# A two-layer mixer kernel: rotated scan states summed on GpSimd before the read, compression with its positions stationary, and four heads' weights per transpose

## What is computed

```python
z = rmsnorm(h, norm_mix) @ w_in              # q, six key/value parts, gates, u
kc, vc = compress(k_cmp, ...), compress(v_cmp, ...)
p_cmp = masked_softmax(q @ kc * scale)       # 31 compressed positions
o = g0 * (p_cmp @ vc) + g1 * o_slc + g2 * o_win

def compress(kv, pe, w1, w2):                # 31 windows of 32 tokens, 2 groups
    return gelu((windows(kv) + pe) @ w1) @ w2   # 2048 -> 256 -> 64

# S5 branch: 32 groups of 16 channels, 64 complex states each
state = scan(a_bar, b_coef * (b @ u))
y = real(state) @ c_re - imag(state) @ c_im + d_skip * u
h = h + concat(o, y_gated) @ w_out
```

## Time and profile before

| | |
|---|---|
| median of 3 runs | 2008.1 us (2006.92 to 2008.7) |
| profiled execution | 2005.77 us, span 2004.0 us |
| granted clock, mean | 0.985 |
| PE, PEld busy | 1936.8 us (97%), 1509.8 us (75%) |
| DVE, ACT, POOL busy | 1185.7 us (59%), 820.9 us (41%), 336.2 us (17%) |
| HBM read | 192.67 MB, 97 GB/s over the span |

### The profile page before, as it was taken

How to read it: one execution, slowest core, us unless ns; L and a number is a source line. 1 busy time by engine, 2 the same in 40 slices (tenths; PEclk the granted TensorE clock), 3 DMA queues, 4 the chain that set the end, 5 groups by cost and what they waited for, 6 DMA issues and landing times.

```text
span 2004.0 us, 22537 instructions
## 1 busy us (share of the span) xinstructions
PE 1936.8 (97%) x9022; PEld 1509.8 (75%) x9022; DVE 1185.7 (59%) x1519; ACT 820.9 (41%) x1210; POOL 336.2 (17%) x329
## 2 busy tenths in 40 slices
PE   7999999999998999999999899999999899999997
PEld 5788888777644788888888778776788778776786
DVE  5748344576764556656655787826753659446732
ACT  5332233311555343213333448545542466445531
POOL 2000000135320110101011212504201024115002
PEclk9999999999998999999999899999999899999998
DMA  5232223222002145645632222221223222221331
GB/s 196 93 106 94 93 96 116 78 74 97 27 1 69 55 151 195 221 141 185 215 111 80 77 93 85 87 95 40 74 95 95 85 82 84 89 80 32 95 98 60
DMA packets 53464, 197.27 MB, mean 98 GB/s; under 512 B 6000, under 2 KB 6512, under 8 KB 52848
## 3 DMA queue, kind: packets, MB, share of 16 engines
q1 hardware_dynamic: 43200, 160.55, 24.4%
q0 software_dynamic: 7648, 29.10, 4.6%
q10 hardware_dynamic: 2512, 6.18, 0.9%
HBM read 192.67 MB, written 2.10 MB: 97 GB/s over the span
## 4 chain that ended last, share of the span: by engine, by line
PE 78%; DVE 13%; ACT 4%; issue 2%; POOL 2%; DMA 1%; ACTq 0%; POOLq 0%; DVEq 0%
PE PS L593 77%; DVE AR L1644 3%; DVE WLO L1641 2%; DVE AR L2170 1%; ACT WHI L1179 1%; DVE AR L1674 1%; DVE TMP L2244 1%; DVE AR L1995 1%; PE PS L843 1%; DVE AR L2137 0%; DMA H<-in_xT 0%; POOL ACC L2302 0%; DVE H L2073 0%; POOL AR L2339 0%; ACT SQ L1194 0%
## 5 line engine op out<-in xcount | busy, mean ns | idle before, releaser
L593 PE MATMUL PS<-HNH,WHI 128*128 128x512 f32 x1632 | 659.3, 404 | 16.4 <-ACT HNH L1210 14.6
L1641 DVE TENSOR_TENSOR WLO<-RAW,WHI 128x1024 fp32r<-128x1024 f32 (+1 forms) x272 | 374.9, 1381 | 506.7 <-ACT WHI L1179 506.6
L593 PE MATMUL PS<-HNH,WLO 128*128 128x512 f32 x1632 | 641.8, 393 | 5.9 <-DVE WLO L1641 5.9
L1179 ACT ACTIVATE WHI<-RAW 128x1024 fp32r<-128x1024 f32 (+1 forms) x272 | 297.7, 1095 | 642.2 <-PE PS L593 583.1
L593 PE MATMUL PS<-HNL,WHI 128*128 128x512 f32 x1632 | 436.3, 391 | 0.1
L593 PEld LDWEIGHTS PS<-HNH,WHI 128*128 128x128 f32 x1632 | 309.1, 189 | 96.3 <-issue 22.1
L593 PEld LDWEIGHTS PS<-HNH,WLO 128*128 128x128 f32 x1632 | 309.5, 190 | 80.4 <-issue 9.1
L593 PEld LDWEIGHTS PS<-HNL,WHI 128*128 128x128 f32 x1632 | 307.6, 188 | 64.8 <-DVE HNL L1644 1.0
L2302 POOL TENSOR_TENSOR ACC<-ACC,SQ 128x512 f32<-128x512 f32 x46 | 62.4, 1356 | 809.8 <-ACT SQ L1194 808.8
L593 PE MATMUL PS<-AR 32*128 32x256 f32 (+14 forms) x844 | 162.3, 414 | 4.4 <-POOL AR L2339 1.7
L593 PE MATMUL PS<-HIDH,WLO 128*128 128x512 f32 x352 | 137.1, 390 | 0.0
(11 more groups left out here) (314 smaller groups left out, 2295.4 us busy)
## 6 DMA issues: line engine op xcount, KB each, us to landing
RAW<-in_w_in SPq DMA_DIRECT2D x80, 512.0 KB, 3.5
AR<-in_w_ada POOLq DMA_DIRECT2D x48, 512.0 KB, 4.1
RAW<-in_w13a SPq DMA_DIRECT2D x44, 512.0 KB, 3.4
RAW<-in_w13b SPq DMA_DIRECT2D x44, 512.0 KB, 3.6
RAW<-in_w_out SPq DMA_DIRECT2D x40, 512.0 KB, 3.5
RAW<-in_w2a SPq DMA_DIRECT2D x16, 704.0 KB, 4.0
RAW<-in_w2b SPq DMA_DIRECT2D x16, 704.0 KB, 5.1
RAW<-in_w_inA SPq DMA_DIRECT2D x12, 512.0 KB, 3.4
```

What stands on the lines that cost most here:

```text
L593: return pe.matmul(o, l, r, start=start, stop=stop, skip_group_check=True)
L1179: act.activation(hi_of(name, i), raw_of(name, i), ACT.Copy).then_inc(*HI.up(name, i))
L1641: dve.tensor_tensor(lo_of(name, i), raw_of(name, i), f32(hi_of(name, i)), S_).then_inc(*LO.up(name, i))
```

## The change

The scan: behind the second `back_v` of each b, POOL adds SQ onto V_, real halves first (`state_re`), imaginary halves second (`state_im`), each over both state tiles (128x2x256). PE's `read` then has two rounds of four matmuls, the first behind `state_re` and the second behind `state_im`. `back` of DVE and POOL no longer waits for PE's read of the b before.

The compression: the 62 positions are the stationary operand, in two column groups (PSUM partitions 0 to 61 and 64 to 125) for the two halves of the weight, which is the moving operand with 128 columns; one bank instead of two. ACT's GELU writes `HIDt`, a new step `hidden` transposes it by two PE matmuls and ACT copies it to `HIDc`. `compressed` for the values comes one n later and writes VC four times, at partitions 0, 32, 64 and 96, with four ACT copies.

The transposes: `ptc` is done for two pairs of heads at once (i = 0 and 2), four transposes of 128 columns into one bank and one ACT copy; `cmp` takes its rows from the partitions 32 x (2 (i % 2) + hf).

The ring of banks turns otherwise from the first `squeeze` on; `out_s5` passes over bank 7.

```diff
     yield "v", z, tt
     if z == 0 and tt < 2:
         yield "turn", 6 + tt
+    if (z, tt) == (0, 1):
+        yield "hidden", 0
     yield from some(1)
 if z == 0:
     yield "compressed", 0
...
 if n < 4:
     yield "squeeze", 1, n
 if n == 4:
+    yield "hidden", 1
+if n == 5:
     yield "compressed", 1
 if 1 < n < 9:
     yield "weigh", n - 2
...
+CET = [CEf.rearrange("p (q a c) -> p q a c", q=4, a=2)[:, :, a, :] for a in range(2)]
...
+HIDt = ar(20800, P)
...
 ps, bY = take(pe, "read", b)
 pe.wait_ge(*V.at("s5_thru", 3))
 mm(ps[slice(64 - r.start, 128 - r.start), 0:HT], THRU[r, y4, r], U[r, y4, 0:HT], True, False)
-for z in range(4):
+for z, (name, wr, wl) in enumerate((("state_re", CpR, CaR), ("state_im", CpI, CaI))):
+    pe.wait_ge(*G.at(name, b))
     for now in (True, False):
         for j in range(2):
             t16 = 2 * b + j
             g = t16 % 4 if now else (t16 + 2) % 4
             o = ps[32 * g:32 * g + 32, 0:HT]
-            wr, wi = (CpR, CpI) if now else (CaR, CaI)
-            if z == 0:
-                pe.wait_ge(*V.at("back_im", t16))
-                w, x = wr, S5T[j][:, HT:T]
-            elif z == 1:
-                pe.wait_ge(*G.at("back_re", t16))
-                w, x = wi, S5T[j][:, 0:HT]
-            elif z == 2:
-                pe.wait_ge(*G.at("back_v", t16))
-                w, x = wr, V_[b % 2][:, j, 0:HT]
+            x = V_[b % 2][:, j, HT * z:HT * z + HT]
+            if now:
+                t = mm(o, wr[:, t16, :], x, z == 0, z == 1)
             else:
-                w, x = wi, V_[b % 2][:, j, HT:T]
-            if now:
-                t = mm(o, w[:, t16, :], x, z == 0, z == 3)
-            else:
-                t = mm(o[:, 1:HT], w[:, t16, :], x[:, 0:HT - 1], False, z == 3)
+                t = mm(o[:, 1:HT], wl[:, t16, :], x[:, 0:HT - 1], False, z == 1)
 t.then_inc(*P_.up("read", b))
 give(bY, V, "read", b)
...
 elif step == "squeeze":
     z, c = at_
     if c == 0:
-        hc_banks[z] = [take(pe, "squeeze", z, mt) for mt in range(2)]
+        hc_banks[z] = take(pe, "squeeze", z)
     name = ("wk1", "wv1")[z]
     w = rows(raw_of(name, c), 256)
     pe.wait_ge(*raw_in(name, c))
     pe.wait_ge(*V.at("positions", z))
-    for mt in range(2):
-        for i in range(4):
-            ii = 4 * c + i
-            t = mm(hc_banks[z][mt][0][:, 0:62], w[:, i, P * mt:P * mt + P],
-                   XBp[:, ii, :, :].rearrange("p g c -> p (g c)"), ii == 0, ii == 15)
+    for i in range(4):
+        ii = 4 * c + i
+        for mt in range(2):
+            t = mm(hc_banks[z][0][64 * mt:64 * mt + 62, 0:P], XBp[:, ii, :, :].rearrange("p g c -> p (g c)"),
+                   w[:, i, P * mt:P * mt + P], ii == 0, ii == 15)
     t.then_inc(*P_.up(name, c))
     if c == 3:
-        for mt in range(2):
-            give(hc_banks[z][mt][1], A, "hidc", z, mt)
+        give(hc_banks[z][1], A, "hidt", z, 1)
+elif step == "hidden":
+    z, = at_
+    for mt in range(2):
+        ps, b = take(pe, "hidden", z, mt)
+        r = slice(64 * mt, 64 * mt + 62)
+        pe.wait_ge(*A.at("hidt", z, mt))
+        pe.transpose(ps[:, 0:62], HIDt[r, :], IDENT[r, r]).then_inc(*P_.up("hidden", z, mt))
+        give(b, A, "hidc", z, mt)
...
 for g in range(2):
     for mt in range(2):
-        t = mm(ps[0:31, 64 * g:64 * g + 64], HIDc[:, mt, 31 * g:31 * g + 31], WV2[:, mt, :], mt == 0, mt == 1)
+        for a in range(2):
+            r = 32 * g + 64 * a
+            t = mm(ps[r:r + 31, 64 * g:64 * g + 64], HIDc[:, mt, 31 * g:31 * g + 31], WV2[:, mt, :], mt == 0, mt == 1)
...
     t.then_inc(*P_.up("shares", i, kind))
     give(b, A, "shares", i, kind)
     out_bank[i, kind] = take(pe, "values", i, kind)
-if part == 0 and kind == 2:
-    for hf in range(2):
-        ps, b = take(pe, "ptc", i, hf)
-        pe.wait_ge(*V.at("weigh", 6))
-        for qt in range(4):
-            t = pe.transpose(ps[0:31, P * qt:P * qt + P], CE[:, qt, 2 * i + hf, 0:31], IDENT)
-        t.then_inc(*P_.up("ptc", i, hf))
-        give(b, A, "ptc", i, hf)
+if part == 0 and kind == 2 and i % 2 == 0:
+    ps, b = take(pe, "ptc", i // 2)
+    pe.wait_ge(*V.at("weigh", 6))
+    for qt in range(4):
+        t = pe.transpose(ps[:, P * qt:P * qt + P], CET[i // 2][:, qt, :], IDENT)
+    t.then_inc(*P_.up("ptc", i // 2))
+    give(b, A, "ptc", i // 2)
 if part == 1 and kind == 2:
     ps, b = take(pe, "cmp", i)
     pe.wait_ge(*A.at("compressed", 1))
     for hf in range(2):
-        pe.wait_ge(*A.at("ptc", i, hf))
-        t = mm(ps[64 * hf:64 * hf + 64, :], VC[0:31, 64 * hf:64 * hf + 64], PTC[hf][0:31, :], True, True)
+        pe.wait_ge(*A.at("ptc", i // 2))
+        r = slice(32 * (2 * (i % 2) + hf), 32 * (2 * (i % 2) + hf) + 31)
+        t = mm(ps[64 * hf:64 * hf + 64, :], VC[r, 64 * hf:64 * hf + 64], PTC[i // 2][r, :], True, True)
     t.then_inc(*P_.up("cmp", i))
     give(b, V, "with_cmp", i)
...
 elif step == "out_s5":
     for m in range(3):
+        if ring[0][0] == 7:
+            ring.append(ring.pop(0))
         w_out_banks[m] = take(pe, "w_out", m)
         w_out(m, (4, 5, 6, 7), True, False)
...
     for mt in range(2 if c == 3 else 0):
         act.wait_ge(*P_.at(("wk1", "wv1")[z], 3))
-        if z:
-            act.wait_ge(*P_.at("compressed", 0))
-        act.activation(HIDc[:, mt, 0:62], bank("squeeze", z, mt)[:, 0:62], ACT.Gelu_apprx_tanh).then_inc(*A.up("hidc", z, mt))
+        r = slice(64 * mt, 64 * mt + 62)
+        act.activation(HIDt[r, :], bank("squeeze", z)[r, 0:P], ACT.Gelu_apprx_tanh).then_inc(*A.up("hidt", z, mt))
+elif step == "hidden":
+    z, = at_
+    for mt in range(2):
+        act.wait_ge(*P_.at("hidden", z, mt))
+        act.activation(HIDc[:, mt, 0:62], bank("hidden", z, mt)[:, 0:62], ACT.Copy).then_inc(*A.up("hidc", z, mt))
 elif step == "compressed":
     z, = at_
     act.wait_ge(*P_.at("compressed", z))
     if z == 0:
         act.activation(KCC[:, 0:62], bank("compressed", 0)[:, 0:62], ACT.Copy).then_inc(*A.up("compressed", 0))
     else:
-        act.activation(VC[0:31, :], bank("compressed", 1)[0:31, 0:128], ACT.Copy).then_inc(*A.up("compressed", 1))
+        for g in range(2):
+            for a in range(2):
+                r = slice(32 * g + 64 * a, 32 * g + 64 * a + 31)
+                act.activation(VC[r, 64 * g:64 * g + 64], bank("compressed", 1)[r, 64 * g:64 * g + 64], ACT.Copy).then_inc(*A.up("compressed", 1))
...
-for hf in range(2 if kind == 2 else 0):
-    act.wait_ge(*P_.at("ptc", i, hf))
-    if i:
-        act.wait_ge(*P_.at("cmp", i - 1))
-    act.activation(PTC[hf][0:31, :], bank("ptc", i, hf)[0:31, :], ACT.Copy).then_inc(*A.up("ptc", i, hf))
+if kind == 2 and i % 2 == 0:
+    act.wait_ge(*P_.at("ptc", i // 2))
+    act.activation(PTC[i // 2], bank("ptc", i // 2)[:, :], ACT.Copy).then_inc(*A.up("ptc", i // 2))
...
 dve.wait_ge(*V.at("scan", b, 1))
 if b < 7:
     dve.wait_ge(*G.at("drive_im", t16 + 2))
-if b:
-    dve.wait_ge(*P_.at("read", b - 1))
 stt(f2(S5T[j][:, HT:T]), f2(V_[b % 2][:, j, HT:T]), -1.0, tables(t16, 2)[1], M_, M_).then_inc(*V.up("back_im", t16))
...
 pool.wait_ge(*V.at("scan", b, 1))
 if b < 7:
     pool.wait_ge(*G.at("drive_im", t16 + 2))
-if b:
-    pool.wait_ge(*P_.at("read", b - 1))
+else:
+    pool.wait_ge(*G.at("state_im", b - 1))
 pool.tensor_tensor(f2(S5T[j][:, 0:HT]), f2(v[:, 0:HT]), s2, M_).then_inc(*G.up("back_re", t16))
 mine()
 pool.wait_ge(*V.at("back_im", t16))
 pool.tensor_tensor(f4(v), f4(v), c4, M_).then_inc(*G.up("back_v", t16))
+if j:
+    v, turned = V_[b % 2], SQ[:, :, :]
+    mine()
+    for z, name in enumerate(("state_re", "state_im")):
+        x = v[:, :, HT * z:HT * z + HT]
+        pool.tensor_tensor(x, x, turned[:, :, HT - HT * z:T - HT * z], A_).then_inc(*G.up(name, b))
```

More of the change, by code:

```diff
@@ L330, in program @@
         RAW = sb("RAW", NSLOT * SLOT)
-        NAR = 20800
+        NAR = 20928
         at_ar = at[0]
```

## The result

| | before | after |
|---|---|---|
| median of the runs, us | 2007.5 | 2027.9 (4 runs, 2024.1 to 2030.0) |
| ratio, 95% interval | 1 | 1.0101 [1.0085, 1.0116] |
| span of the profiled execution, us | 2004.0 | 2025.5 |
| granted clock, mean over the span | 0.985 | 0.975 |
| PE busy, us | 1936.8 (97%) | 1933.9 (95%) |

The change makes the kernel 20 us slower. Slower was forecast, but 2027.9 lies above the range's 2024. PE did not gain its "some 10 us" of busy time: 140 matmuls fewer took 2.9 us less.

A forecast was written before the change was run, and what follows sets the result against it. PE, busy 97% of the span, was taken as the bound, but POOL's products set the end at five of eight reads. Terms gave +5.4 us, plus 3.5 for the clock: +8.9 on the median 2008.1, so 2017.0, range 1998 to 2024.

The forecast's parts named there:

- bank of read 2: Read 2 waits for the bank DVE frees with turn 6 and ends at 496.7 instead of 493.8: +2.9 us.
- lower clock behind the waits: PE's waits at reads 1, 2, 6, 7 could lower the clock, 1.75 us each; two of four counted: +3.5.
- the sums' own time in PE's path, read halved: PE waits for two POOL adds per read: +0.9 at read 0, +9.8 for five reads, -0.5 at reads 3, 4.
- POOL's additions slow DVE, and the clock with it: Sixteen adds could slow DVE by up to 12.8 us; only two beside positions counted, 1.6 within read 2's bank.
- the array's part, its saving: Six shorter squeezes -4.8 us, fewer transposes -3.1, added work +0.6, drive 7's short bank wait swallowed -0.4.
- The term for read 0: With the sums read 0 ends at 442.4 against 441.6 now, stated as +0.9 us.
- all four waits: By the skill's text the clock falls at reads 1, 2, 6 and 7 alike: +7.0 us instead of +3.5.
- the adds are hidden: Rival, faster: the DVE and POOL chain moves forward with PE, which finds the sums ready; 1995 to 1998 us; chance 0.20.
- bank and clock don't bite: Rival, same: turn 6's bank in time, DVE not slowed, clock unaffected by 3 us waits; +2.5, 2010.6 us; chance 0.20.
- the clock falls each time: Rival, slower: the clock falls after all four waits, reads 1, 2, 6, 7; +12.4, 2020.5 us; chance 0.15.
- the column groups of squeeze run one after the other: Rival, slower: squeeze's two column groups don't overlap, so its saving is 0; 2022 us; chance 0.05.
- what would show it: Profile signs: PE waits 12 to 18 us for adds, squeezes 1.1 us, PE busy some 10 us less, clock below 1.

The follow-up runs named there:

- experiment 9: Changed kernel with the bank ring turned two places before read 2 and accumulating matmuls in all PE waits for the sums: 2015.9 us, 1.0053.
- experiment 10: Changed kernel without the sums, ring turned before read 2, plus two unread POOL additions behind each b from 0 to 6: 2007.6 us, 1.0005.
- 5: Changed kernel with only the ring of PSUM banks turned by two places before read 2: 2024.8 us, 1.0084.
- 7: Changed kernel without the sums (read of before) and with the bank ring turned two places before read 2: 1999.2 us, 0.9962.
- Experiment 8: Kernel before with the read's matmuls halved, no sums added, part of the state left out of y: 2007.2 us, 1.0007.
- 3: Kernel before plus two POOL additions of 128x512 that nobody reads, behind the last product of each b from 0 to 6: 2014.3 us, 1.0041.
- experiment 6: Changed kernel with matmuls with a start flag in PE's waits for the sums, read 2's bank wait left: 2020.9 us, 1.0068.
- Experiment 2: Kernel before with only the sums on POOL and the halved read: 2026.3 us, 1.0098.
- experiment 1: Changed kernel without the sums, read of before; the new squeeze and four heads per transpose stay: 2006.2 us, 0.9998.

## Why the prediction was too low

The runs make a ladder from the changed kernel to the best one, each step the difference of two ratios, beside the terms of the sum. The step from 9 to 10 takes the sums out of the read, with PE's waits and the matmuls in them, and leaves as many additions on POOL (fourteen for sixteen) that nobody reads. Each step is uncertain by 4 to 5 us (the last by 2.5), so the first isn't clear of noise:

| step | runs | measured, us | forecast, us |
|---|---|---|---|
| bank of read 2 | after to 5 | 3.4 | 2.9 |
| lower clock behind the waits | 5 to 9 | 6.2 | 3.5 |
| the sums' own time in PE's path, read halved | 9 to 10 | 9.6 | 0.9 + 9.8 - 0.5 = 10.2 |
| POOL's additions slow DVE, and the clock with it | 10 to 7 | 8.6 | 0, but for 1.6 inside the bank's term |
| the array's part, its saving | 7 to before | -7.6 | -4.8 - 3.1 + 0.6 - 0.4 = -7.7 |
| together | | 20.2 | 8.9 |

**What held.** That PE doesn't find the sums done, and roughly the size of it: the third step is within its error of what was forecast. It is a mixed step, though. The matmuls in the waits keep the mean clock at 0.985 in experiment 9, and without them experiment 10 has 0.982. What is clean is the step from 9 to 7, both at 0.985 and without the late bank: 18.3 us for the sums, own time and contention together, where the forecast has 10.2 and 1.6. The split of it into 9.6 and 8.6 is not. At most reads an addition takes 1.25 to 1.36 us, against 1.27 in the sum. At read 1 the two took 3.46, since WLO and the scans run beside them (0.9 us that the sum didn't have). Squeeze took 1.09, as forecast, four heads' weights 0.66 where half of 1.06 was taken, and two small transposes 0.27; the worth of it all, 7.6 us (5 to 10 by its interval), is as forecast once the bank is out of the way. Experiment 8 fits the statement that at most of the reads POOL sets the end, though the lower clock in it would hide a saving too. The term for read 0 is 0.8 by its own figures (442.4 - 441.6), not 0.9. The bank at read 2 was named, with its place and releaser.

**The step that failed: "The sum takes only the two that meet positions, since elsewhere DVE has idle time or reads PSUM."** Experiments 3 and 10 measure 8.2 and 8.6 us for fourteen additions nobody waits for, the lower clock that comes along included. DVE's idle time is there, but it lies behind the scans, not under the additions. POOL's last product of a read and DVE's next scan of four begin together, and the additions follow the product into the scan. At read 5 of the changed kernel DVE's scan goes from 556.42 to 560.9, and POOL's timeline has beside it:

```profile
556.65 1.26 POOL L2349 TENSOR_TENSOR AR<-AR 128x512 f32<-128x512 f32 x1 [2.44 <-DVE SQ L1656]
557.99 2.60 POOL L2355 TENSOR_TENSOR AR<-AR,SQ 128x512 f32<-128x512 f32 x2
```

A scan stands between one drive and the next states, and at reads 4 to 6 its delay of 1.6 us is found again in everything behind it (experiment 10). Where PE waits longer by it, the clock can fall as well. The price per operation was read rightly, 0.8 us for each POOL operation; it was multiplied by two where fourteen were due: 14 x 0.8 = 11, and in experiment 10 the scans and the positions grew by 8.3 and 1.5, 9.8 together. The Trainium skill ("GPSIMD Engine Reference", section "Key points") was quoted in the prediction for just this contention on two-input instructions, with up to 12.8 us; the trace agrees with it, and I argued it away on DVE's idle share, an average over a stretch.

**The term that was mis-sized: "I count two of the four: +3.5."** The granted clock fell behind seven reads (all but read 3), and the matmuls in the waits give back 6.2 to 6.6 us. Rows 9 and 10 were read as a bound, "after 1.95 us idle the clock stayed at 1.00". That wait stood between 128x512 matmuls with no gap among them. At read 0, behind two waits of 0.90 and 0.59 us with a pair of light matmuls ahead of them and eight column-tiled ones between, the clock was at 0.50 in the window 442 to 446 us. The light work alone doesn't bring it down: the kernel before has 48 such pieces without a wait at that place and 1.00, and experiment 6, with matmuls in the waits, has 1.00 too. Nor do the waits settle it. Experiment 2 has the same pieces in the same order there, with waits of 0.91 and 0.59 us, and kept the full clock:

```profile
439.38 2.56 PE L593 MATMUL PS<-AR 128*32 128x256 f32 x24 [0.59 <-POOL AR L2333]
...
442.00:446.00 4.00, 4.00 (x18) 3.30 (x19) 4.00 (x7) 0.00 (x0) 1.53 (x1) 1.00 0.00 0
```

So one sequence came out at either level, and neither the length of a wait nor the work around it told which; what decides stays open. The Trainium skill ("TensorE: Matmul & The Clock Gate", section "HAM oscillation") speaks of a wait long enough between bursts. The prediction's reading of it, all four waits, gave +7.0, and that is the nearer figure. But the fall behind the short waits of read 0 is not of that kind, and the places are other ones.

**The bank.** The place and the term were right, its reason only in part. The forecast made the bank late because the sums slow the positions. In experiment 1, which has no sums, the bank is 6.9 us late all the same, because PE comes to read 2 long before DVE reaches turn 6. So it took from the array's part what it saved: experiments 1 and 7 differ by 7.2 us. By the forecast's terms, 7.7 of saving and 2.9 of bank, 4.8 us net would be left without the sums; experiment 1 shows 0.4 (0.9998).

**The rivals.** That the adds are hidden fell: eleven waits name them. That bank and clock don't bite fell. That the clock falls each time came true and more, behind seven reads where it counted four; its 2020.5 lacked the contention. That the column groups of squeeze run one after the other fell: 1.09 us. Of "what would show it", PE's busy time was wrong: it fell by 2.9 us, not 10, with the matmuls behind most waits at the lower level (0.63 us for 0.40 at read 0).

## What to carry to other kernels

An addition moved to a spare engine was paid three times here: in its own time if somebody waits for it, in the other engine's instructions that run beside it, and in the clock of the engine that waits. Before such a move, put the timeline of the two vector engines side by side at each place and multiply the slowdown per operation by all operations that meet a chain, whatever the idle share says. After any edit that changes how many banks are held, look who frees the bank of each step behind it: two lines that turn the ring were worth 7.2 us here (experiments 1 and 7), and the array's whole part is worth 7.6 only with them in. And time a kernel several times before a small gain is believed: experiment 10 has executions 14 us apart, the shortest ones at the highest granted clock.

## What the runs showed that was not expected

- Useless matmuls in waits made the kernel 6.6 us faster (experiment 6, its output changed) and 6.2 (experiment 9 against 5, its output intact).
- The granted clock fell to 0.50 after waits of 0.90 and 0.59 us at read 0 of the changed kernel. It stayed at 1.00 after the same waits in experiment 2, and after 1.95 us elsewhere.
- Two POOL additions of two inputs lengthen a DVE scan of four by 1.6 us (2.41 to 4.01) when they read another tile than DVE's, and by 2.0 (4.45) when they are the real sums: POOL needn't touch the same tile. The unread ones, which write one scratch tile, took 1.08 us each (2.15 for two at 527.31) and the real ones 1.31.
